# A two-block transformer kernel on one core: the second attention's keys and queries computed token-major

## The reference

```python
def rms_norm_2(x, g):
    y = xf * lax.rsqrt(jnp.mean(xf * xf, axis=-1, keepdims=True) + EPS)
    return (y * g.astype(jnp.float32)).astype(x.dtype)

def rope(x, cos, sin):                      # cos, sin: (T, 64)
    x1, x2 = xf[..., :half], xf[..., half:]
    return jnp.concatenate([x1 * c - x2 * s, x2 * c + x1 * s], axis=-1).astype(x.dtype)
...
k, v = jnp.split(hn @ w_kv, 2, axis=-1)
k = rope(rms_norm_2(k.reshape(B, T, N_HEADS, HEAD_DIM_2), k_norm), cos, sin)
...
q = (h @ w_q[j]).reshape(B, T, N_HEADS, HEAD_DIM_2)
q = rope(rms_norm_2(q, q_norm[j]), cos, sin).transpose(0, 2, 1, 3)
...
s_own = jnp.einsum('bhqd,bhkd->bhqk', qc, k_own).astype(jnp.float32) * sm_scale
```

## Time and profile before

| | us |
|---|---|
| median of three runs | 1389.29 |
| profiled execution | 1389.15 |
| its span in the trace | 1387.4 |
| TensorE busy | 1342.5 (97%) |
| VectorE busy | 928.1 (67%) |
| ScalarE busy | 656.0 (47%) |
| mean granted TensorE clock | 0.99 of full speed |

### The profile page before, as it was taken

The page is one execution under the profiler, slowest core; times in us unless marked ns, Lnnn a source line. Parts: engine busy times, 40 slices in busy tenths (PEclk is TensorE's granted clock), DMA queues, the critical chain, the costliest instruction groups (busy, mean ns, idle before and its releaser), DMA issues.

```text
span 1387.4 us, 16653 instructions
## 1 busy us (share of the span) xinstructions
PE 1342.5 (97%) x6785; PEld 1105.5 (80%) x6785; DVE 928.1 (67%) x1012; ACT 656.0 (47%) x849; POOL 24.6 (2%) x49
## 2 busy tenths in 40 slices
PE   8999899999998999998999999999999998999998
PEld 8976577888886888887788888878888886788887
DVE  5467788766668776667776677576666756744454
ACT  5356666545457333445444436453444545644432
POOL 2200000000000000000000000000000000000000
PEclk9999999999999999999999999999999999999999
DMA  9997569677774887773877773667778441455651
GB/s 251 253 330 227 155 239 357 232 275 273 274 270 168 301 288 273 273 242 122 286 272 281 282 273 106 215 224 260 273 276 308 143 133 51 151 194 188 192 184 61
DMA packets 165567, 317.54 MB, mean 229 GB/s; under 512 B 7018, under 2 KB 114852, under 8 KB 156276
## 3 DMA queue, kind: packets, MB, share of 16 engines
q1 hardware_dynamic: 161872, 305.50, 64.7%
q0 software_dynamic: 3440, 10.93, 2.8%
q10 hardware_dynamic: 180, 0.05, 0.0%
HBM read 314.10 MB, written 1.84 MB: 228 GB/s over the span
## 4 chain that ended last, share of the span: by engine, by line
PE 87%; DVE 7%; ACT 3%; issue 2%; DMA 1%; ACTq 0%; SPq 0%; DVEq 0%
PE bank L715 27%; PE bank L717 26%; PE bank L716 26%; PE bank L812 2%; DVE full L1836 2%; PE bank L735 1%; DVE wlo L1769 1%; PE bank L738 1%; DMA raw<-in_w_in 1%; DVE xt L1824 1%; DVE mix L1822 1%; PE bank L762 1%; DMA raw<-in_w_mlp_in 1%; PE bank L1076 1%; ACT whi L1348 1%
## 5 line engine op out<-in xcount | busy, mean ns | idle before, releaser
L1769 DVE TENSOR_TENSOR wlo<-raw,whi 128x2048 fp32r<-128x2048 f32 x205 | 469.2, 2290 | 262.6 <-ACT whi L1348 262.3
L1348 ACT ACTIVATE whi<-raw 128x2048 fp32r<-128x2048 f32 x205 | 392.3, 1914 | 216.3 <-PE bank L717 179.3
L715 PE MATMUL bank<-whi,uhi 128*128 128x512 f32 (+2 forms) x1088 | 429.4, 395 | 12.5 <-DVE ulo L1849 4.6
L717 PE MATMUL bank<-whi,ulo 128*128 128x512 f32 (+2 forms) x1088 | 419.9, 386 | 0.0
L716 PE MATMUL bank<-wlo,uhi 128*128 128x512 f32 (+2 forms) x1088 | 418.8, 385 | 0.0
L715 PEld LDWEIGHTS bank<-whi,uhi 128*128 128x128 f32 x1088 | 206.1, 189 | 60.2 <-issue 17.2
L717 PEld LDWEIGHTS bank<-whi,ulo 128*128 128x128 f32 x1088 | 206.0, 189 | 42.0
L716 PEld LDWEIGHTS bank<-wlo,uhi 128*128 128x128 f32 x1088 | 206.5, 190 | 39.7 <-issue 1.2
L715 PE MATMUL bank<-whi,hsplit 128*128 128x512 f32 (+1 forms) x512 | 200.9, 392 | 1.1 <-DVE wlo L1769 1.1
L717 PE MATMUL bank<-whi,hsplit 128*128 128x512 f32 (+1 forms) x512 | 198.5, 388 | 0.0
L716 PE MATMUL bank<-wlo,hsplit 128*128 128x512 f32 (+1 forms) x512 | 198.3, 387 | 0.0
(11 more groups left out here) (253 smaller groups left out, 1026.0 us busy)
## 6 DMA issues: line engine op xcount, KB each, us to landing
raw<-in_ffn_w_in SPq DMA_DIRECT2D x176, 512.0 KB, 4.8
ada<-in_ada_w SPq DMA_DIRECT2D x72, 1024.0 KB, 7.2
raw<-in_ffn_w_out SPq DMA_DIRECT2D x44, 1024.0 KB, 5.1
raw<-in_w_in SPq DMA_DIRECT2D x16, 1024.0 KB, 10.7
raw<-in_w_mlp_in SPq DMA_DIRECT2D x16, 1024.0 KB, 6.8
raw<-in_w_mlp_out SPq DMA_DIRECT2D x16, 1024.0 KB, 5.0
ada<-in_kv_ada_w SPq DMA_DIRECT2D x8, 1024.0 KB, 7.3
raw<-in_w_kv SPq DMA_DIRECT2D x8, 1024.0 KB, 5.3
```

The lines of the kernel that those rows point to most:

```text
L715: nc.tensor.matmul(o, sh, mh, start=start, stop=False, skip_group_check=skip)
L717: return nc.tensor.matmul(o, sl, mh, start=False, stop=stop, skip_group_check=skip)
L1348: ins = nc.scalar.activation(whi[:, ring(n), :], raw[:, ring(n), :], ACT.Copy)
L1769: ins = nc.vector.tensor_tensor(wlo[:, ring(n), :], raw[:, ring(n), :], whi[:, ring(n), :].bitcast(F32), ALU.subtract)
```

## The change

- Keys and queries 0-511 come from 512-column slots with tokens stationary, queries 512-1023 from two 256-column slots with tokens stationary (`q_slot`). All come out with tokens on partitions. In kv the keys are now slots b to b+3 and the values b+4 to b+7. The stage wq begins with `first_chunk` as the other stages do, and two calls of `keep_busy` in wq and one in kv (12 transposes) go.
- Keys: ScalarE squares each head with a sum along the row (`k_part`), takes roots of 128x4, and copies each head scaled by its root. VectorE rotates (`rotate`: two operations on half heads, two on whole, for four heads of one token tile). TensorE transposes pairs of heads (`turn_heads`, four transposes of 128x128), and ScalarE copies them out (`heads_copy`).
- Queries: ScalarE copies them out raw, VectorE rotates them, TensorE transposes, ScalarE copies. The inverse roots, times minus 128 to the power -0.5, are not multiplied in: they are handed to the attention's VectorE operation as its scale for a row of scores (`q_scale`), which was the constant -1.0.
- The norm gains are multiplied into the cos and sin tables (`gains_on_angles`, two operations of 128x256 in ffn1 and in ffn2), for which GpSimd's queue loads the tables twice and each gain in three DMAs. Two small loads on ScalarE's queue at the start and the permutation matrix go.
- `head_sums`, `swap_halves`, `rotary_copy`, `rotary_root` and `rotary` go (their text and their calls on ScalarE and VectorE are left out below).

```diff
+                c0, h = 512 * (n // 2), n % 2
+                slot(START["kv"] + n, v4, w_kv[:, 4 * h:4 * h + 4, c0:c0 + 512])
...
+            for n in range(2):
+                slot(START["wq"] + n, v4, w_q[:, 4 * n:4 * n + 4, 0:512])
+            for n in range(2, 4):
                 slot(START["wq"] + n, v8, w_q[:, :, 256 * n:256 * n + 256])
...
+            def rotary_tables(gain):
+                pool.dma_start(cst[:, CST["cos"][0]:], cst_dram[:, CST["cos"][0]:]).then_inc(rotary_in, 16)
+                pool.dma_start(turned1[:, 0:P], gain.partition_broadcast(P)).then_inc(rotary_in, 16)
+                pool.dma_start(turned1[:, P:P + 64], gain[64:P].partition_broadcast(P)).then_inc(rotary_in, 16)
+                pool.dma_start(turned1[:, P + 64:2 * P], gain[0:64].partition_broadcast(P)).then_inc(rotary_in, 16)
...
+            def turn_heads(p, src, o, done):
+                for h in range(2):
+                    for t in range(2):
+                        ins = nc.tensor.transpose(o[:, h * T + t * P:h * T + (t + 1) * P],
+                                                  src[:, t, (2 * p + h) * P:(2 * p + h + 1) * P], ident)
+                ins.then_inc(done, 1)
...
             b = START["kv"]
             first_chunk(b, 5, bank[4:6])
-            keep_busy(12, bank[6])
-            for q in range(4):
-                pe.wait_ge(u2_full, q + 1)
-                wide8(b + 2 + q, bank[q])
-                if q > 1:
-                    swap_halves(0, q - 2)
-                if q > 0:
-                    head_sums(0, q - 1)
-            u_slot(b + 6, 0, bank[6:8])
-            swap_halves(0, 2)
-            head_sums(0, 3)
-            u_slot(b + 7, 1, bank[6:8])
-            swap_halves(0, 3)
+            window_taken(5)
+            u_slot(b + 2, 0, bank[6:8])
+            u_slot(b + 3, 1, bank[6:8])
+            pe.wait_ge(u2_full, 4)
+            u_slot(b + 4, 0, bank[0:2])
+            pe.wait_ge(k_rotated, 2)
+            for p in (0, 1):
+                turn_heads(p, k_t, bank[4 + p], k_turned)
+            u_slot(b + 5, 1, bank[0:2])
+            u_slot(b + 6, 0, bank[2:4])
+            pe.wait_ge(k_rotated, 4)
+            for p in (2, 3):
+                turn_heads(p, k_t, bank[4 + p], k_turned)
+            u_slot(b + 7, 1, bank[2:4])
             ffn("ffn2", None)
 
+            def q_slot(n, o):
+                pe.wait_ge(lo_done, n + 1)
+                for t in range(2):
+                    for k in range(KT):
+                        ins = mm3(o[:, t * T:(t + 1) * T], uhi[:, k, tokens(t)], ulo[:, k, tokens(t)],
+                                  v8(whi, n)[:, k, :], v8(wlo, n)[:, k, :], k == 0, k == KT - 1)
+                ins.then_inc(pe_done, 1)
+                piece(n)
             b = START["wq"]
-            window(6, 0)
...
-            keep_busy(8, bank[3])
-            turn_u(6, 1)
-            pe.wait_ge(u_lo, 26)
-            keep_busy(10, bank[1])
-            for q in range(4):
-                wide8(b + q, bank[q], u_at=24 if q == 0 else None)
-                if q > 1:
-                    swap_halves(1, q - 2)
-                if q > 0:
-                    head_sums(1, q - 1)
-            head_sums(1, 3)
+            first_chunk(b, 6, bank[0:2])
+            q_slot(b + 2, bank[2])
+            pe.wait_ge(q_rotated, 2)
+            for p in (0, 1):
+                turn_heads(p, q_t, bank[p], q_turned)
+            q_slot(b + 3, bank[3])
+            pe.wait_ge(q_rotated, 3)
+            turn_heads(2, q_t, bank[2], q_turned)
 
             def last_heads(u):
-                if u < 2:
-                    swap_halves(1, 2 + u)
+                if u == 3:
+                    pe.wait_ge(q_rotated, 4)
+                    turn_heads(3, q_t, bank[3], q_turned)
 
             def rotated(u):
-                pe.wait_ge(r_done, 4 + u // 2 + 1)
+                pe.wait_ge(q_done, u // 2 + 1)
...
+            def k_part(c, t):
+                src, dst = bank[4 + 2 * c + t], k_t[:, t, 512 * c:512 * c + 512]
+                for h in range(4):
+                    s = slice(h * P, (h + 1) * P)
+                    ins = nc.scalar.activation(dst[:, s], src[:, s], ACT.Square, accum_out=k_sum[:, t, 4 * c + h:4 * c + h + 1])
+                link(ins)
+                roots = k_root_of[:, t, 4 * c:4 * c + 4]
+                link(nc.scalar.activation(roots, k_sum[:, t, 4 * c:4 * c + 4], ACT.Ln, bias=eps[:], scale=1.0 / P))
+                link(nc.scalar.activation(roots, roots, ACT.Exp, scale=-0.5))
+                for h in range(4):
+                    s = slice(h * P, (h + 1) * P)
+                    ins = nc.scalar.activation(dst[:, s], src[:, s], ACT.Copy, scale=k_root_of[:, t, 4 * c + h:4 * c + h + 1])
+                ins.then_inc(k_taken, 1)
+            def heads_copy(p, dst, src, turned, done):
+                act.wait_ge(turned, p + 1)
+                nc.scalar.activation(dst[:, 2 * p:2 * p + 2, :], src[:], ACT.Copy).then_inc(done, 1)
+            def q_roots(h0, count, parts):
+                for t, src in parts:
+                    nc.scalar.activation(q_raw[:, t, h0 * P:(h0 + count) * P], src, ACT.Copy).then_inc(q_taken, 1)
+                act.wait_ge(q_taken, max(h0, 2))
+                for t in range(2):
+                    for h in range(h0, h0 + count):
+                        ins = nc.scalar.activation(q_junk[:, t, h * P:(h + 1) * P], q_raw[:, t, h * P:(h + 1) * P], ACT.Square,
+                                                   accum_out=q_scale[:, t, h:h + 1])
+                link(ins)
+                q = q_scale[:, :, h0:h0 + count]
+                link(nc.scalar.activation(q, q, ACT.Ln, bias=eps[:], scale=1.0 / P))
+                link(nc.scalar.activation(q, q, ACT.Exp, scale=-0.5))
+                nc.scalar.activation(q, q, ACT.Copy, scale=-P ** -0.5).then_inc(q_root, 1)
...
             conv(b + 3)
             act.wait_ge(pe_done, b + 2)
+            k_part(0, 0)
+            conv(b + 4)
+            k_part(0, 1)
+            conv(b + 5)
+            act.wait_ge(pe_done, b + 4)
+            k_part(1, 0)
+            conv(b + 6)
+            k_part(1, 1)
+            conv(b + 7)
+            for p in (0, 1):
+                heads_copy(p, k2, bank[4 + p], k_turned, k_done)
+            act.wait_ge(pe_done, b + 6)
             take_v(0)
...
+            conv(b + 8)
             act.wait_ge(pe_done, b + 7)
             act.wait_ge(u2_full, 4)
             u2_high(0)
             conv(b + 9)
...
+            for p in (2, 3):
+                heads_copy(p, k2, bank[4 + p], k_turned, k_done)
             conv(b + 10)
             u2_high(1)
...
+            conv(b + 3)
+            act.wait_ge(pe_done, b + 2)
+            act.wait_ge(ada_used, N_JOBS)
+            q_roots(0, 4, [(t, bank[t][:]) for t in range(2)])
+            conv(b + 4)
+            for p in (0, 1):
+                heads_copy(p, q2, bank[p], q_turned, q_done)
+            act.wait_ge(pe_done, b + 3)
+            q_roots(4, 2, [(t, bank[2][:, t * T:(t + 1) * T]) for t in range(2)])
+            conv(b + 5)
+            heads_copy(2, q2, bank[2], q_turned, q_done)
             conv(b + 6)
...
             def o_between(u):
+                if u == 1:
+                    q_roots(6, 2, [(t, bank[3][:, t * T:(t + 1) * T]) for t in range(2)])
+                if u == 3:
+                    heads_copy(3, q2, bank[3], q_turned, q_done)
...
+            def gains_on_angles(r):
+                dve.wait_ge(rotary_in, 64 * (r + 1))
+                for angles, g in ((cos_t, 0), (sin_t, 1)):
+                    link(nc.vector.tensor_tensor(angles, angles, gain_rows[:, g:g + 1, :].to_broadcast([P, 2, P]), ALU.mult))
...
+            def rotate(dst, src, turned, cos, sin):
+                nc.vector.tensor_tensor(turned[..., 0:64], src[..., 64:P], sin[..., 0:64], ALU.mult)
+                link(nc.vector.tensor_tensor(turned[..., 64:P], src[..., 0:64], sin[..., 64:P], ALU.mult))
+                link(nc.vector.tensor_tensor(dst, src, cos, ALU.mult))
+                return nc.vector.tensor_tensor(dst, dst, turned, ALU.add)
...
+            def rotate_four(t, c, dst, src):
+                s = slice(512 * c, 512 * c + 512)
+                return rotate(four_heads(dst[:, t, s]), four_heads(src), four_heads(turned_t[:, t, s]),
+                              cos_t[:, t:t + 1, :].to_broadcast([P, 4, P]), sin_t[:, t:t + 1, :].to_broadcast([P, 4, P]))
+            def rotate_keys(c, t):
+                dve.wait_ge(k_taken, 2 * c + t + 1)
+                rotate_four(t, c, k_t, k_t[:, t, 512 * c:512 * c + 512]).then_inc(k_rotated, 1)
...
 
...
 
...
+            conv(b + 3)
+            rotate_keys(0, 0)
+            conv(b + 4)
+            rotate_keys(0, 1)
+            conv(b + 5)
+            rotate_keys(1, 0)
+            conv(b + 6)
+            rotate_keys(1, 1)
             conv(b + 7)
...
             conv(b + 8)
             u2_low(0)
...
             conv(b + 9)
             conv(b + 10)
```

(27 more changed lines are left out.)

124 lines of the change are left out of this document (34 added, 90 removed).

## The result

| | before | changed |
| --- | --- | --- |
| median, us (executions timed together) | 1389.55 (4) | 1378.12 (4; 1376.59 to 1380.09) |
| ratio, 95% interval | | 0.9927 [0.9913, 0.9941] |
| profiled execution / its span, us | 1389.15 / 1387.4 | 1380.09 / 1378.0 |
| mean granted clock of that execution | 0.990 | 0.986 |

Forecast 1375.0 in 1370.5 to 1381: the sign and the size are right, and 3.1 us are missing. The median lies 0.1 above 1372.5 to 1378, the range of the forecast without its rivals. The profiled execution was the slowest of the four.

What follows compares the result with a forecast made beforehand. TensorE bounds the kernel (87% of the span), except the attention, set by the heads' chain through VectorE and ScalarE. 1389.15 - 5.6 (kv) - 9.4 (wq, attention) + 0.8 (clock) = 1375.0; range 1370.5 to 1381, without rivals 1372.5 to 1378.

Steps and rivals of the forecast that it cites:

- kv, 5.6: In kv, 512-column slots without sums and swaps, rotations hidden, hand-over to ffn2 unchanged at 6.9: gains 5.6 us.
- wq and attention, 9.4: Earlier first slots in wq and one rotation instead of two in the attention end it at 1158.2, 9.4 us earlier.
- Rotation and small operations: VectorE's rotation of four heads priced at 2.1 us, ScalarE's 128x128 operation with sum at 0.38 at most.
- rival 3: Slower: rotation by strided half heads in kv, wq and attention at three times the price, 6.3 us; 1396; chance 0.03.
- Rival 1: ScalarE's small query operations take 0.5, not 0.38, and bind; wq gives 4 to 6; 1379 to 1381; chance 0.17.
- Rival 4: The change does not free TensorE: feeding binds in kv with slots at 5.45; 1383 to 1386; chance 0.03.
- The clock, +0.8: Half of one 3 us half-clock stretch on TensorE, after kv's new idle time or in wq: 0.8 us, ends 0 and 3.0.
- The Trainium skill: Half clock is TensorE's default; if kv's new idle time surely costs one stretch, the sum is 0.7 us higher.

Runs made afterwards that it cites:

- after_third: The changed kernel run once more with no edit, on a third chip; median 1378.64 us, ratio 0.9920 to the kernel before.
- keys_only: Against the kernel before, only kv's keys changed, queries and their rotations as before, 12 transposes still out; median 1386.61 us, ratio 0.9985.
- keys_busy: Against the kernel before, only the keys changed, with the 12 keep_busy transposes in kv back; median 1382.81 us, ratio 0.9960.
- two_busy: The changed kernel with the 12 keep_busy transposes back in kv and keep_busy transposes added in the attention; median 1374.26 us, ratio 0.9902.

## Why the prediction came out, and what it missed

- **kv, 5.6.** Right, by its own steps: slots of 5.47 (5.45 said), `turn_heads` at 0.40 to 0.44 (0.44), the hand-over to ffn2 of 6.9 unchanged. Measured 5.47 at equal clock. (The terms of the forecast add up to 5.5 and, for the arithmetic on TensorE alone, 6.4, not the 5.6 and 6.5 written.) The sums and swaps were on the path, and the rotations are hidden with 7.4 us of slack (5 to 7 said).
- **wq and attention, 9.4.** The pattern is right: tile 0 behind the pieces, tile 1 4.03 later, no wait of TensorE for a rotation. At the clock of before wq gives 8.1 (42.74 - 34.66, 8.3 said). The attention at full clock gives 0.9 (1.1 said), but that sets it against a kernel before with 3.4 us at half clock. With the same 3.4 us (after_third, 23.10) it gives 0.1.
- **Rotation and small operations.** 2.14 (2.1 said), which closes rival 3. ScalarE's squares go at 0.29 from start to start, below the 0.38 that I used as an upper price:

```profile
1121.22 0.30 ACT L1699 ACTIVATE ada<-ada 128x128 f32<-128x128 f32 x1
...
1121.51 0.29 ACT L1699 ACTIVATE ada<-ada 128x128 f32<-128x128 f32 x1
```

  The scale as a pointer costs what was priced, 480 ns against 419:

```profile
L2330 DVE CUSTOM_DVE_ANT_0 mix<-bank,cst,small 128x256 f32<-128x256 f32 x8 | 3.8, 480 | 0.0
```

  Rival 1 gave the same 1379 to 1381 as the profiled execution by another way, and is refuted: TensorE waits for no rotation, and the first exponential starts 2.5 us behind the first scores. Rival 4 falls with the slots at 5.47.
- **The clock, +0.8: the term that was mis-sized.** The three traces of the changed kernel have 124.34, 125.00 and 126.04 where the same work at 63.86, 34.66 and 22.37 takes 120.89: 3.5, 4.1 and 5.2 us of clock. That is beyond the upper end of 3.0. I had counted one stretch of 3 us and named the keys and the first query slots for it; the attention, whose row at 0.50 stood in my own list, I had put together from VectorE's operations, with no wait for a TensorE at half clock: the sum thereby took out the old stretch for nothing, where the three traces have 3.4 to 10.2 us of it. And the stretches were longer than the 3 us that I priced at 1.5: 6.8 us in kv, both times, cost 2.8, and 6.8 us at the start of wq cost 3.3 (36.3 against 33.0). In the median, 1378.12 against the 1374.2 of the sum without its clock term, 3.9 us are missing: the 9 us more at half clock make 2.4 of them at 0.27 each, 0.4 lie outside the span, and about 1 us is not explained.
- **The Trainium skill** (TensorE: Matmul & The Clock Gate, The HAM clock gate) has the half clock as the default that sustained work lifts. Read as a price on every new idle time, it would have put my sum 0.7 higher and nearer. The runs give that reading only in part: the gap of 2.8 us cost its stretch in two traces of six.

What stays open: why the whole change has 8 to 10 us more half clock, when each half of it with the 12 transposes has no more than the kernel before; why two fillers lower it together and hardly apart; and what decides in which execution a stretch falls on the start of wq. No run forced it to fall or stay away there. The 1.6 us of the first stage were not tested; they are absent from the second and the third trace.

## What to carry to other kernels

Work taken off the path leaves idle time at the places where other engines are awaited. List these places, look at the granted clock of each in the trace, and price a low stretch by the dense work behind it, before counting the gain. Removing filler work with the work that it stood beside can go with the loss of more than half of the gain (1.8 us of median in keys_only, 6.0 with the filler in keys_busy), and one trace will not show it: compare the mean granted clock over all executions, and fit the time against it. Tell first which engine releases which at the clock that is granted: moving VectorE's conversion gave nothing at half clock and 0.6 us at full.

## What the runs showed of the hardware

- The clock can fall without idle time. At the start of wq TensorE is busy without a break (7.00 of 7.00 us), but with two groups of 16 single-column sums ahead; in the changed kernel's trace the clock is at 0.51 there; in the trace of two_busy, with the same code in this place, the same four multiplications go at full clock (3.76 us and 1.96).
- The same idle time of 2.84 to 2.89 us ahead of a dense stream cost nothing in four traces and 2.8 us in two. Filled down to between 1.53 and 1.56 us it cost nothing in any of the eight traces that have it so, the kernel before among them.
- A dense stream of 512 columns runs at 0.427 us a multiplication at 1.2 GHz and 0.227 at 2.4 GHz, 1.88 times as much: nearly the whole spacing scales with the clock.
- Over 116 executions that differed by themselves, 1 us more at half clock went with 0.27 us more time on the mean; single stretches cost more where dense work fell in them (2.8 us for 6.8 in kv, 3.3 for 6.8 at the start of wq).
